# Recurrence of a state space mixer: order of drives, turned inputs and kernel products, and the last state additions handed to TensorE

## The chip, the cores and the metric

One Trainium2 chip, one of its cores. The metric is the device time of one execution in microseconds; lower is better.

## What is computed

Two transformer-like blocks on 256 positions of width 1024, all in float32. The change touches only the first mixer of the first block, a diagonal complex state space model (S5): 512 inner channels in 32 groups of 16, each group with 64 complex states.

```python
u = (h @ w_in).reshape(bsz, seq, SSM_GROUPS, SSM_CH)
mag = jnp.exp(lr * dt)
abar_re = mag * jnp.cos(li * dt)
abar_im = mag * jnp.sin(li * dt)
bu_re = jnp.einsum('bsgc,gpc->bsgp', u, bbar_re)
bu_im = jnp.einsum('bsgc,gpc->bsgp', u, bbar_im)
_, _, xs_re, xs_im = lax.associative_scan(combine, (a_re, a_im, bu_re, bu_im), axis=1)
# y = real part of (c * xs) plus d_skip * u, then gelu, a gate, and w_out
```

After it come a squared-ReLU MLP, an attention mixer with a top-k index, another MLP, and the second block (an SSD branch, windowed attention, a gated MLP). All of that follows in order behind the mixer and is the same before and after.

## The kernel before

The program is written out per engine: each engine has one hand-written stream, in which every instruction stands where it will run, and semaphores (`pe.wait_ge(S(name), n)`, `.then_inc(S(name), 1)`) tie the streams. Nothing reorders them. Weights stream in as numbered pieces in a ring: SyncE loads a piece into `raw`, ScalarE rounds it to `HI`, VectorE and GpSimd make the rest `LO = raw - HI`, and TensorE multiplies with both. `keep_busy(o, n)` issues n products of zeros (bf16, 512 columns) that write into an unused PSUM stretch; they compute nothing.

The recurrence is done in chunks of CL = 4 steps, so there are NC = 64 chunks, and 16 pairs of groups (`ST` tiles) in four quarters q of four tiles. Its steps, with the engine and the names:

- `ch_major` (TensorE): the two pieces of `ssm_w_in`, which give the channels `u`. `to_steps` (ScalarE) rearranges them into `ush`, and SyncE spreads them with 32 small transfers (line 375) into `u5` (in the tile `y`): sixteen for the first half of the channels (`u5_in0`), sixteen for the second (`u5_in1`).
- `inputs_turned(g)` (TensorE, line 778): four transposes of a quarter of the input weights `w5`; `inputs_out` (ScalarE, line 1545) copies them out to `wt5`. Eight such g, through two PSUM banks, so that g waits for the copy of g - 2.
- `drive(q)` (TensorE, line 785): eight products that give the inputs of the chunk states of quarter q.
- `kernels5` (TensorE, line 794): 32 products that give the kernels inside a chunk, with a last product that adds the skip term (line 798, `kk_psum`). ScalarE copies them to `m5` (line 1590, ten copies, `m5_ready`), behind its copies of `cq5` (line 1581), of which the second pair waits for both `u5_in0` and `u5_in1`, since `cq5` lies over `ush`.
- `scanned(q)` (VectorE, lines 2192 to 2202): ten instructions. Two turn the inputs by the angles in `e5`, two add, two are the scans along the chunks, two turn the states back into four products (`ra` and `rb`, 512 columns each), and two (lines 2201 and 2202) add those in pairs to the real and the imaginary part. Then `x5_ready`.
- `within(q)` (TensorE, line 806): the outputs of a chunk from its own inputs, after `m5_ready`. `carried(q)` (TensorE, line 814): the outputs from the state carried into the chunk, after `x5_ready`; 32 products on 32 columns of the array each.
- Gelu on ScalarE (line 1602), the gate `glu`, and the two pieces of `ssm_w_out` (`down`, line 707), then the norm and the first MLP.

What decides the order around the change is thus the text of the TensorE, ScalarE and VectorE streams, and SyncE's single queue of 32 transfers.

## Time and profile before

| | us |
|---|---|
| median of 3 runs (1314.05 to 1314.8) | 1314.8 |
| the profiled execution, its own time | 1318.43 |
| its span | 1316.6 |
| TensorE busy | 1256.2 (95%) |
| VectorE busy | 950.8 (72%) |
| ScalarE busy | 672.3 (51%) |
| GpSimd busy | 424.5 (32%) |
| mean granted TensorE clock | 0.986 of full |

The span runs from the first to the last instruction of the profiled execution; its own time is 1.8 us longer, and taken with the profiler on. The mixer's recurrence lies in the first 92 us of the span. Busy shares are means over the whole program, and say little on so short a stretch; the views of single stretches do. Times within a view are microseconds from the start of the span.

### The profile page before, as it was taken

To read this page: it belongs to the slowest core of one execution; us is meant where nothing else is said; L and a number is where in the kernel's file an instruction comes from. 1 tells how busy PE (TensorE), PEld (TensorE's weight loads), DVE (VectorE), ACT (ScalarE), POOL (GpSimd) and SP (SyncE) were. 2 spreads that over 40 slices of the span, in tenths; PEclk is the share of its full clock that TensorE was granted. 3 is DMA by queue.
4 is the path that set the end of the run, shared out by engine and by line. 5 is a ranking of instruction groups with operands and counts; after the bars stand their busy time and mean duration, and the time that the engine had idled before them with its cause. 6 is when DMAs were issued, how large, how long until landed. Compare 5 with 4: busy or idle time off the path is not lost.

```text
span 1316.6 us, 21079 instructions
## 1 busy us (share of the span) xinstructions
PE 1256.2 (95%) x7823; PEld 1072.4 (81%) x7850; DVE 950.8 (72%) x1439; ACT 672.3 (51%) x1103; POOL 424.5 (32%) x217
## 2 busy tenths in 40 slices
PE   6999999998889999999999999999999999999998
PEld 5866888876667688888788888798999967899997
DVE  7776777676775665556686755468999875799997
ACT  5565444444455444444464544356556643555553
POOL 3014444544211455554344322100000013344543
PEclk9999999999989999999999999999999999999999
DMA  7045665645212566665366533255445514366663
GB/s 231 16 140 182 187 196 178 199 143 175 81 65 80 163 193 191 188 190 150 114 222 192 160 97 97 65 147 161 150 151 159 160 62 146 104 190 189 191 190 112
DMA packets 168927, 197.61 MB, mean 150 GB/s; under 512 B 12542, under 2 KB 133886, under 8 KB 168830
## 3 DMA queue, kind: packets, MB, share of 16 engines
q1 hardware_dynamic: 167499, 192.01, 47.6%
q10 hardware_dynamic: 1362, 4.74, 1.0%
q8 instruction: 41, 0.67, 0.2%
q14 instruction: 25, 0.20, 0.0%
HBM read 195.14 MB, written 1.05 MB: 149 GB/s over the span
## 4 chain that ended last, share of the span: by engine, by line
PE 74%; DVE 13%; DMA 5%; ACT 5%; issue 2%; POOL 1%; SPq 0%; DVEq 0%; ACTq 0%
PE acc L707 23%; PE wk L659 9%; PE wk L621 7%; PE wk L622 7%; PE wk L623 7%; PE wk L661 5%; DMA raw<-in_w_in 2%; DVE LO L475 2%; PE wk L1193 1%; ACT HI L1438 1%; PE acc L926 1%; PE acc L1219 1%; PE acc L621 1%; PE acc L622 1%; PE acc L623 1%
## 5 line engine op out<-in xcount | busy, mean ns | idle before, releaser
L475 POOL TENSOR_TENSOR LO<-raw,HI 128x1024 fp32r<-128x1024 f32 (+1 forms) x158 | 393.4, 2496 | 568.8 <-ACT HI L1438 500.0
L1438 ACT ACTIVATE HI<-raw 128x1024 fp32r<-128x1024 f32 (+3 forms) x382 | 366.1, 995 | 132.9 <-PE acc L707 38.7
L475 DVE TENSOR_TENSOR LO<-raw,HI 128x1024 fp32r<-128x1024 f32 (+1 forms) x156 | 222.7, 1431 | 84.6 <-ACT HI L1438 84.2
L621 PE MATMUL wk<-X,HI 128*128 128x256 f32 x784 | 225.2, 287 | 4.1 <-ACT arena L1872 1.7
L622 PE MATMUL wk<-X,HI 128*128 128x256 f32 x784 | 222.5, 284 | 0.0
L623 PE MATMUL wk<-X,LO 128*128 128x256 f32 x784 | 222.4, 284 | 0.0
L659 PE MATMUL wk<-X,HI 128*128 128x512 f32 x512 | 183.7, 401 | 2.5 <-DVE X L2024 2.5
L621 PEld LDWEIGHTS wk<-X,HI 128*128 128x128 f32 x784 | 150.8, 192 | 7.9 <-issue 3.3
L622 PEld LDWEIGHTS wk<-X,HI 128*128 128x128 f32 x784 | 150.9, 193 | 1.0
L623 PEld LDWEIGHTS wk<-X,LO 128*128 128x128 f32 x784 | 150.9, 193 | 0.0
L661 PE MATMUL wk<-X,LO 128*128 128x256 f32 x512 | 144.1, 281 | 0.0
L707 PE MATMUL acc<-HI,HH 128*128 128x512 f32 x392 | 122.5, 394 | 0.7 <-DVE HL L2518 0.7
L707 PE MATMUL acc<-LO,HH 128*128 128x512 f32 x392 | 121.2, 390 | 0.0
L707 PE MATMUL acc<-HI,HL 128*128 128x512 f32 x392 | 120.9, 390 | 0.0
L659 PEld LDWEIGHTS wk<-X,HI 128*128 128x128 f32 x512 | 96.9, 189 | 26.6 <-issue 2.9
L661 PEld LDWEIGHTS wk<-X,LO 128*128 128x128 f32 x512 | 97.3, 190 | 1.1
L1991 DVE TENSOR_TENSOR LO<-raw,HI 128x1024 fp32r<-128x1024 f32 x68 | 80.2, 1219 | 10.9 <-ACT HI L1438 10.3
L621 PE MATMUL wk<-HI,X 128*128 128x512 f32 x208 | 83.5, 401 | 4.2 <-DVE X L2024 4.2
L707 PEld LDWEIGHTS acc<-LO,HH 128*128 128x128 f32 x392 | 73.6, 188 | 16.0
L707 PEld LDWEIGHTS acc<-HI,HL 128*128 128x128 f32 x392 | 73.6, 188 | 15.8
L2277 DVE TENSOR_TENSOR HL<-arena,HH 128x512 fp32r<-128x512 f32 x32 | 84.0, 2625 | 2.8 <-ACT HH L1635 2.8
L622 PE MATMUL wk<-LO,X 128*128 128x512 f32 x208 | 81.8, 393 | 0.0
(393 smaller groups left out, 2077.1 us busy)
## 6 DMA issues: line engine op xcount, KB each, us to landing
raw<-in_mlp_w SPq DMA_DIRECT2D x128, 512.0 KB, 4.1
raw<-in_w_in SPq DMA_DIRECT2D x100, 512.0 KB, 4.4
raw<-in_w_up SPq DMA_DIRECT2D x44, 512.0 KB, 4.0
raw<-in_w_down SPq DMA_DIRECT2D x44, 256.0 KB, 3.2
raw<-in_att_w_in SPq DMA_DIRECT2D x16, 512.0 KB, 4.1
raw<-in_w_ssd_proj SPq DMA_DIRECT2D x16, 512.0 KB, 3.6
raw<-in_att_w_out SPq DMA_DIRECT2D x8, 512.0 KB, 3.6
raw<-in_w_out SPq DMA_DIRECT2D x8, 512.0 KB, 4.1
```

The source lines that it names most:

```text
L475: tensor_tensor(LO[:, s, cs], raw[:, s % 2, "ab".index(part), 0:m], HI[:, s, cs].bitcast(F32), ALU.subtract).then_inc(S(f"lo_{part}"), 1)
L621: mm(o, lh, rh, start=start, stop=False, skip_group_check=skip)
L622: mm(o, lh, rl, start=False, stop=False, skip_group_check=skip)
L623: return mm(o, ll, rh, start=False, stop=stop, skip_group_check=skip)
L659: mm(o, HI[:, s, w:w + P], X2[:, k, :, :].rearrange("p r t -> p (r t)"), start=k == 0, stop=False, skip_group_check=True)
L661: last = mm(o[:, 0:SEQ], LO[:, s, w:w + P], XH[:, k, :], start=False, stop=k == KD - 1, skip_group_check=True)
L707: last = mm(acc[:, tb, n * 512:(n + 1) * 512], lhs[:, ts], w[:, s, c:c + 512], start=begin, stop=end, skip_group_check=True)
L926: last = mm(acc[:, tb, n * 512:(n + 1) * 512], lhs[:, par, kk, ts], w[:, slots[par], c:c + 512], start=False, stop=end, skip_group_check=True)
L1193: last = mm(wkf[:, o:o + K], qT2[hs, gi * 4 + hd // 2, tb * P:(tb + 1) * P], kT2[hs, gi * 4 + hd // 2, 0:K], start=True, stop=True)
L1438: A(HI[:, s, j * m:(j + 1) * m], raw[:, s % 2, j, 0:m], ACT.Copy).then_inc(S(f"hi_{part}"), 1)
L1991: TT(LO[:, s, cs], raw[:, s % 2, "ab".index(part), :], HI[:, s, cs].bitcast(F32), ALU.subtract).then_inc(S(f"lo_{part}"), 1)
L2277: TT(HL[:, par, :, :], sq_b[:, par, :].rearrange("p (j t) -> p j t", j=2), HH[:, par, :, :].bitcast(F32), ALU.subtract).then_inc(S("hid_lo ...
```

## The change

TensorE's stream: the two first `inputs_turned` no longer stand inside the second `ch_major` but behind it, and the eight are taken as pairs by quarter (real and imaginary part of q together) instead of all real ones first. Between the pairs stand drives and quarters of `kernels5`, with two of the `keep_busy` products that stood there left. Drives 0 and 1 and all of `kernels5` stand ahead of drives 2 and 3; 18 `keep_busy` products follow drive 3, where 8 did. `carried(q)` takes four products per state instead of two sums: 64 instructions instead of 32. VectorE's `scanned(q)` loses its two last additions, and the copy of a plane of `e5` (line 2179) goes too. ScalarE makes the three planes of `e5` with one Copy more, ahead of six of the eight `inputs_out`, and all eight of them now stand ahead of the `cq5` copies. The exponential of `alog` moves from ahead of the first Gelu to behind the `z2_hi` copies.

```diff
@@ -770,7 +770,7 @@
             def inputs_turned(g):
-                r, q = g // 4, g % 4
+                q, r = g // 2, g % 2
                 pe.wait_ge(S("w5_ready"), r + 1)
                 if g >= 2:
                     pe.wait_ge(S("bt_ready"), g - 1)
@@ -786,15 +786,16 @@
                                   u5[:, 4 * q + a, :], start=True, stop=True)
                 last.then_inc(S("bu_psum"), 1)
-            def kernels5(half):
-                for i in range(8 * half, 8 * half + 8):
-                    keep_busy(spare5, 1)
+            def kernels5(q):
+                for i in range(4 * q, 4 * q + 4):
                     for r in range(2):
                         mm(accf[:, 1536 + i * 32:1568 + i * 32], w5[:, r, i, :], ct5[:, r, i, :], start=(i == 0 and r == 0),
                            stop=False, skip_group_check=True)
-                if half == 0:
-                    return
+            def skip_added():
+                pe.wait_ge(S("dd5_ready"), 1)
                 mm(accf[0:32, 1536:2048], ident[0:32, 0:32], dd5.rearrange("p i n -> p (i n)"), start=False, stop=True,
                    skip_group_check=True).then_inc(S("kk_psum"), 1)
@@ -809,11 +810,11 @@
             def carried(q):
                 pe.wait_ge(S("x5_ready"), q + 1)
-                for o, r in itertools.product(range(CL), range(2)):
+                for o, r, part in itertools.product(range(CL), range(2), range(2)):
                     for j in range(4):
                         last = mm(accf[32 * j:32 * j + 32, Y5[q] + o * NC + 1:Y5[q] + (o + 1) * NC],
-                                  cq5[:, r, 4 * q + j, 32 * o:32 * o + 32], lp[:, q, r, j * NC:(j + 1) * NC - 1],
-                                  start=False, stop=(r == 1), skip_group_check=True)
+                                  cq5[:, r, 4 * q + j, 32 * o:32 * o + 32], lp[:, q, r, part * 256 + j * NC:part * 256 + (j + 1) * NC - 1],
+                                  start=False, stop=(r == 1 and part == 1), skip_group_check=True)
                 last.then_inc(S("x5_used"), 1)
             def glu(s, k):
@@ -830,31 +831,34 @@
             spare5 = accf[:, 1024:1536]
-            def first_inputs():
-                pe.wait_ge(S("ct_ready"), 1)
-                pe.wait_ge(S("cols_ready"), 2)
-                inputs_turned(0)
-                inputs_turned(1)
-            used(ch_major(arrived(), 1, between=first_inputs))
-            for g in range(2, 8):
-                keep_busy(spare5, 2)
-                inputs_turned(g)
+            def turned_pair(q):
+                inputs_turned(2 * q)
+                inputs_turned(2 * q + 1)
+            used(ch_major(arrived(), 1))
+            pe.wait_ge(S("ct_ready"), 1)
+            pe.wait_ge(S("cols_ready"), 2)
+            turned_pair(0)
+            kernels5(0)
+            keep_busy(spare5, 2)
+            turned_pair(1)
             pe.wait_ge(S("u5_in0"), 16 * 16)
+            drive(0)
+            kernels5(1)
+            turned_pair(2)
+            pe.wait_ge(S("bt_ready"), 4)
+            drive(1)
+            kernels5(2)
+            turned_pair(3)
+            kernels5(3)
+            skip_added()
+            pe.wait_ge(S("u5_in1"), 16 * 16)
+            pe.wait_ge(S("bt_ready"), 8)
+            drive(2)
             keep_busy(spare5, 2)
-            pe.wait_ge(S("bt_ready"), 8)
-            drive(0)
-            keep_busy(spare5, 1)
-            drive(1)
-            kernels5(0)
-            pe.wait_ge(S("dd5_ready"), 1)
-            kernels5(1)
-            pe.wait_ge(S("u5_in1"), 16 * 16)
-            for q in range(2, 4):
-                keep_busy(spare5, 1)
-                drive(q)
-            keep_busy(spare5, 8)
+            drive(3)
+            keep_busy(spare5, 18)
             pe.wait_ge(S("m5_ready"), 1)
             pe.wait_ge(S("m5_zero"), 3)
             for q in range(4):
@@ -1540,9 +1544,10 @@
                 last.then_inc(S("w5_ready"), 1)
             def inputs_out(first, end):
-                for r, q in ((g // 4, g % 4) for g in range(first, end)):
-                    act.wait_ge(S("bt_psum"), 4 * r + q + 1)
-                    A(wt5[:, 4 * q:4 * q + 4, r, :], wk[:, 2 + q % 2, :].rearrange("p (a n) -> p a n", a=4), ACT.Copy)\
+                for g in range(first, end):
+                    q, r = g // 2, g % 2
+                    act.wait_ge(S("bt_psum"), g + 1)
+                    A(wt5[:, 4 * q:4 * q + 4, r, :], wk[:, 2 + r, :].rearrange("p (a n) -> p a n", a=4), ACT.Copy)\
                         .then_inc(S("bt_ready"), 1)
             act.wait_ge(S("ct_psum"), 1)
@@ -1563,15 +1568,16 @@
                 last = A(cols[:, 1 + r, 0:n], wk[:, 3, r * P:r * P + n], ACT.Copy)
             last.then_inc(S("cols_ready"), 1)
             padded(1)
+            to_steps(1)
             inputs_out(0, 2)
-            to_steps(1)
-            inputs_out(2, 4)
             act.wait_ge(S("angle5_part"), 3)
             A(e5[:, :, 2, :], e5[:, :, 1, :], ACT.Abs).then_inc(S("turn5_abs"), 1)
-            A(e5[:, :, 1, :], e5[:, :, 1, :], ACT.Sin, scale=float(2 * np.pi))
+            steps.link(A(e5[:, :, 0, :], e5[:, :, 1, :], ACT.Sin, scale=float(2 * np.pi)))
             act.wait_ge(S("turn5_abs"), 1)
-            A(e5[:, :, 0, :], e5[:, :, 2, :], ACT.Sin, scale=float(-2 * np.pi), bias=sm5[:, 12, 0:1]).then_inc(S("e5_ready"), 1)
-            inputs_out(4, 8)
+            A(e5[:, :, 1, :], e5[:, :, 2, :], ACT.Sin, scale=float(-2 * np.pi), bias=sm5[:, 12, 0:1]).then_inc(S("turn5_abs"), 1)
+            act.wait_ge(S("turn5_abs"), 2)
+            A(e5[:, :, 2, :], e5[:, :, 0, :], ACT.Copy, scale=-1.0).then_inc(S("e5_ready"), 1)
+            inputs_out(2, 8)
             for r in range(2):
                 act.wait_ge(S("q5_half"), r + 1)
                 if r == 1:
@@ -1592,9 +1598,6 @@
             act.wait_ge(S("q5_ready"), 1)
             load_gpre(1)
             hi_to(3)
-            act.wait_ge(S("late_in"), 16 * N_LATE)
-            A(alog[:, :], alog[:, :], ACT.Exp).then_inc(S("alog_ready"), 1)
             for first, end in ((0, 2), (2, 3), (3, 4)):
                 act.wait_ge(S("x5_used"), end)
                 act.wait_ge(S("x5_ready"), end)
@@ -1617,6 +1620,8 @@
                 A(XH[:, 4 + 2 * b:6 + 2 * b, :].rearrange("p q (c t) -> p q c t", t=CL),
                   z2f[:, 2 * b:2 * b + 2, :].rearrange("p q (t c) -> p q c t", t=CL), ACT.Copy, scale=0.5)\
                     .then_inc(S("z2_hi"), 1)
+            act.wait_ge(S("late_in"), 16 * N_LATE)
+            A(alog[:, :], alog[:, :], ACT.Exp).then_inc(S("alog_ready"), 1)
             hi_to(6)
             post(1, 4)
@@ -2176,7 +2181,6 @@
                 link(TT(grid(qb), by_power(pw5[:, 1, 1:5, :]), every_power(cc5[:, 1 - r, :, :]), ALU.mult))
                 TT(qa, qa, qb, ALU.add if r == 0 else ALU.subtract).then_inc(S("q5_half"), 1)
             dve.wait_ge(S("e5_ready"), 1)
-            link(V.tensor_copy(e5[:, :, 2, :], e5[:, :, 0, :]))
             dve.wait_ge(S("mag4_ready"), 1)
             def planes(t):
@@ -2188,18 +2192,16 @@
                 ps = slice(4 * q, 4 * q + 4)
                 ra, rb, z = lp[:, q, 0, :], lp[:, q, 1, :], z5
                 bu = wk[:, q, :].rearrange("p (a r c) -> p r a c", a=4, r=2)
-                ea, eb = (e5[:, ps, n:n + 2, :].rearrange("p a r c -> p r a c") for n in range(2))
+                eb, ea = (e5[:, ps, n:n + 2, :].rearrange("p a r c -> p r a c") for n in range(2))
                 TT(planes(ra), bu, ea, ALU.mult)
                 link(TT(planes(rb), bu, eb, ALU.mult))
-                TT(ra[:, 0:256], ra[:, 0:256], ra[:, 256:512], ALU.add)
+                TT(ra[:, 0:256], ra[:, 0:256], ra[:, 256:512], ALU.subtract)
                 link(TT(rb[:, 0:256], rb[:, 256:512], rb[:, 0:256], ALU.subtract))
                 mag = mag4[:, ps, :].rearrange("p a c -> p (a c)")
                 V.tensor_tensor_scan(z[:, 0:256], mag, ra[:, 0:256], 0.0, ALU.mult, ALU.add)
                 link(V.tensor_tensor_scan(z[:, 256:512], mag, rb[:, 0:256], 0.0, ALU.mult, ALU.add))
                 TT(planes(ra), planes(z), ea, ALU.mult)
-                link(TT(planes(rb), planes(z), eb, ALU.mult))
-                TT(ra[:, 0:256], ra[:, 0:256], ra[:, 256:512], ALU.subtract)
-                TT(rb[:, 0:256], rb[:, 0:256], rb[:, 256:512], ALU.add).then_inc(S("x5_ready"), 1)
+                TT(planes(rb), planes(z), eb, ALU.mult).then_inc(S("x5_ready"), 1)
             def z_low(first, end):
                 bs = slice(first, end)
```

TensorE, from the end of the second input projection to its first gate products: L621 to L623 are the projection, L778 the transposes, L686 `keep_busy`, L785 a drive, L794 and L798 kernel products and skip term before the change. The piece below, in the order before, is from the last transposes to the first kernel products; the pattern of its last two rows goes on until all 16 tiles are done.

```order
L778 MATMUL wk<-cst,arena 128x128 x4
L686 MATMUL acc<-zero_bf 128x512 x2
L778 MATMUL wk<-cst,arena 128x128 x4
L686 MATMUL acc<-zero_bf 128x512 x2
L785 MATMUL wk<-y,arena 128x64 x8
L686 MATMUL acc<-zero_bf 128x512
L785 MATMUL wk<-y,arena 128x64 x8
L686 MATMUL acc<-zero_bf 128x512
L794 MATMUL acc<-arena 128x32 x2
L686 MATMUL acc<-zero_bf 128x512
L794 MATMUL acc<-arena 128x32 x2
```

The same stretch of TensorE after the change, from the first transposes to the skip term; L793 and L799 are what L794 and L798 were.

```order
L778 MATMUL wk<-cst,arena 128x128 x8
L793 MATMUL acc<-arena 128x32 x8
L686 MATMUL acc<-zero_bf 128x512 x2
L778 MATMUL wk<-cst,arena 128x128 x8
L785 MATMUL wk<-y,arena 128x64 x8
L793 MATMUL acc<-arena 128x32 x8
L778 MATMUL wk<-cst,arena 128x128 x8
L785 MATMUL wk<-y,arena 128x64 x8
L793 MATMUL acc<-arena 128x32 x8
L778 MATMUL wk<-cst,arena 128x128 x8
L793 MATMUL acc<-arena 128x32 x8
L799 MATMUL acc<-arena,cst 32x512
```

What moved: the transposes left the projection, kernel products now stand between transposes and drives in fours of tiles, and drives 2 and 3 come behind the skip term. The next piece is TensorE right behind drive 3, at the chunk outputs (L806 and L807 `within`, L814 and L815 `carried`), before:

```order
L785 MATMUL wk<-y,arena 128x64 x8
L686 MATMUL acc<-zero_bf 128x512 x8
L806 MATMUL acc<-y,arena 32x64 x16
...
L806 MATMUL acc<-y,arena 32x64 x16
L686 MATMUL acc<-zero_bf 128x512
L814 MATMUL acc<-arena 32x63 x32
L686 MATMUL acc<-zero_bf 128x512
```

TensorE at the same place after the change:

```order
L785 MATMUL wk<-y,arena 128x64 x8
L686 MATMUL acc<-zero_bf 128x512 x18
L807 MATMUL acc<-y,arena 32x64 x16
...
L807 MATMUL acc<-y,arena 32x64 x16
L686 MATMUL acc<-zero_bf 128x512
L815 MATMUL acc<-arena 32x63 x64
L686 MATMUL acc<-zero_bf 128x512
```

The filler behind the drives grew, and each carried step doubled its products, with the same shapes. On ScalarE, around the input copies (L1545 and L1550 `inputs_out`, L1570 to L1573 and L1574 to L1579 the planes of `e5`, L1581 and L1587 `cq5`), before:

```order
L1545 ACTIVATE arena<-wk 128x4x128 x2
L1531 ACTIVATE arena<-wk 128x512
L1545 ACTIVATE arena<-wk 128x4x128 x2
L1570 ACTIVATE arena<-arena 128x16x64
L1571 ACTIVATE arena<-arena 128x16x64
L1573 ACTIVATE arena<-arena 128x16x64
L1545 ACTIVATE arena<-wk 128x4x128 x4
L1581 ACTIVATE arena<-arena,cst 128x64x16 x2
L1581 ACTIVATE arena<-gpre,cst 128x64x16 x2
L1590 ACTIVATE arena<-acc 32x16x32 x10
```

ScalarE at the same place after the change, with one row of the other projection ahead:

```order
L1535 ACTIVATE arena<-wk 128x512
L1550 ACTIVATE arena<-wk 128x4x128 x2
L1574 ACTIVATE arena<-arena 128x16x64
L1575 ACTIVATE arena<-arena 128x16x64
L1577 ACTIVATE arena<-arena 128x16x64
L1579 ACTIVATE arena<-arena 128x16x64
L1550 ACTIVATE arena<-wk 128x4x128 x6
L1587 ACTIVATE arena<-arena,cst 128x64x16 x2
L1587 ACTIVATE arena<-gpre,cst 128x64x16 x2
```

The planes of `e5` now stand ahead of six of the input copies, and a fourth instruction joins them.

## Rows read from the trace of the kernel before

**Rows 1.** The chain of waits that ended last, 60 to 90 us: start, length, what.

```profile
61.06 0.98 PE acc L798 x2
...
68.10 0.65 PE acc L806 x32
...
71.79 1.02 PE acc L814 x64
...
75.64 1.02 PE acc L814 x64
...
83.67 1.06 PE acc L814 x64
84.76 0.39 ACT arena L1602
```

**Rows 2.** Timeline of TensorE: start, length, line, count of records, idle before.

```profile
34.55 1.03 PE L778 MATMUL wk<-cst,arena 128*128 128x128 f32 x8
...
38.52 0.38 PE L686 MATMUL acc<-zero_bf 128*128 128x512 bf16 x1
...
44.40 0.63 PE L778 MATMUL wk<-cst,arena 128*128 128x128 f32 x4 [2.02 <-ACT arena L1545]
...
51.83 0.53 PE L794 MATMUL acc<-arena 128*128 128x32 f32 x4
...
62.19 3.84 PE L785 MATMUL wk<-y,arena 128*128 128x64 f32 x32
65.86 1.89 PE L686 MATMUL acc<-zero_bf 128*128 128x512 bf16 x8
...
73.06 0.52 PE L814 MATMUL acc<-arena 128*32 128x63 f32 x21 [0.25 <-issue]
73.83 0.85 PE L814 MATMUL acc<-arena 128*32 128x63 f32 x43 [0.24 <-issue]
```

**Rows 3.** The 32 transfers into `u5`: issue times and lengths in ns, time to landing.

```profile
L375 SPq DMA_DIRECT2D y<-arena x32: 593/597/1117, 30.8 to 51.3; - x32
...
DMA to landing us min/median/max: 1.8/1.8/2.6
```

**Rows 4.** Timeline of ScalarE, 40 to 95 us.

```profile
46.70 0.60 ACT L1545 ACTIVATE arena<-wk 128x512 f32<-128x512 f32 x1 [1.04 <-PE wk L778]
47.20 2.17 ACT L1581 ACTIVATE arena<-arena,cst 128x1024 f32<-128x1024 f32 x2
53.21 2.19 ACT L1581 ACTIVATE arena<-gpre,cst 128x1024 f32<-128x1024 f32 x2 [3.84 <-DMA y<-arena]
...
73.53 1.28 ACT L1602 ACT_TABLE_LOAD   x1
...
92.46 1.06 ACT L1438 ACTIVATE HI<-raw 128x1024 fp32r<-128x1024 f32 x1 [0.93 <-DMA raw<-in_mlp_w]
```

**Rows 5.** Timeline of VectorE, 45 to 95 us.

```profile
45.18 0.69 DVE L2179 COPY arena<-arena 128x1024 f32<-128x1024 f32 x1
49.97 0.69 DVE L2192 TENSOR_TENSOR arena<-wk,arena 128x512 f32<-128x512 f32 x1 [4.10 <-PE wk L785]
...
54.72 0.42 DVE L2201 TENSOR_TENSOR arena<-arena 128x256 f32<-128x256 f32 x1
...
83.03 0.42 DVE L2202 TENSOR_TENSOR arena<-arena 128x256 f32<-128x256 f32 x1
...
93.95 1.22 DVE L475 TENSOR_TENSOR LO<-raw,HI 128x1024 fp32r<-128x1024 f32 x1
```

**Rows 6.** Windows: length, busy us of each engine (count), granted clock, DMA share, GB/s.

```profile
41.60:45.00 3.40, 1.38 (x11) 0.85 (x9) 3.33 (x4) 3.15 (x5) 0.00 (x0) 1.00 0.12 24
45.00:48.40 3.40, 3.40 (x14) 2.22 (x12) 0.86 (x2) 2.29 (x4) 0.00 (x0) 0.50 0.13 29
...
62.10:65.50 3.40, 3.35 (x30) 3.35 (x31) 1.35 (x3) 3.34 (x6) 2.82 (x3) 1.00 0.00 0
...
113.30:116.70 3.40, 3.23 (x10) 2.77 (x11) 2.37 (x4) 3.40 (x4) 1.41 (x1) 0.51 0.85 302
```

## The prediction

> **What bounds the kernel now.** I read the chain of waits that ended last first, because busy shares over 1316 us say nothing on a stretch of 60 us. Between 60 and 90 us it alternates: the skip term on TensorE ends at 62.04, then ten ScalarE copies into `m5` fill the time until `within` starts at 68.10, then TensorE alone leads through `within`, the carried steps at 71.79 and 75.64, the gate products, and the last carried step at 83.67, after which Gelu starts at 84.76 [rows 1]. So two things set the end of the recurrence: when `m5` is ready, and the sum of TensorE's work behind it. Next the timelines of the three engines. TensorE stood idle for 2.02 us before 44.40, since the copies of the turned inputs stood behind the `e5` instructions on ScalarE, and its first kernel product came at 51.83 [rows 2]. ScalarE had its `cq5` copies done at 55.40, the second pair having waited 3.84 us for the transfers into `u5`, and from 55.40 to 62.06 it waited for TensorE [rows 4, 1]. VectorE waited 4.10 us for drive 0 and began at 49.97 [rows 5].
>
> **Part 1, `m5` earlier.** What is due first is drive 0, and it needs the first sixteen transfers. 32 are issued evenly from 30.8 to 51.3, one each 0.66 us, and each lands 1.8 us after its issue [rows 3]: the sixteenth at 30.8 + 15 x 0.66 + 1.8 = 42.5, the last at 53.1. Nothing in the change moves these. TensorE's projection ended by 38.5; without eight transposes (1.03, of which 0.15 overlaps) it ends at 37.6 [rows 2]. Then come transposes, a quarter of the kernel products, two fillers and transposes, until 41.3, and TensorE idles some 1.2 us for the transfers. From 42.5 on it runs drive 0, kernels, transposes, drive 1, kernels, transposes. Prices: two drives with a filler between took 3.84, and a filler 0.22 (eight in 1.89), so 1.85 a drive [rows 2]; sixteen tiles of kernel products with sixteen fillers took 61.06 - 51.83 = 9.23, so 0.58 a tile, 0.36 without the filler, 1.45 a quarter [rows 1, 2]; eight transposes 0.87. The sum is 2 x (1.85 + 1.45 + 0.87) = 8.3, and the last transposes end at 50.8, with 0.2 for seams at 51.0. ScalarE's copies keep up: its planes of `e5` are three instructions on 1024 columns and now a fourth, at the 1.05 that each such copy into `cq5` takes [rows 4], from 39.1 to some 43.4, and the next transposes ask for a copy only at 45.8.
>
> Behind 51.0 ScalarE has a last input copy (0.5 until the next may start), two pairs of `cq5` copies of 2.1 (the second could start at 53.7, after 53.1, so it no longer waits), and the ten `m5` copies, which took 62.04 to 68.10 = 6.05 [rows 1, 4]. 51.0 + 0.1 + 0.5 + 4.2 + 6.0 = 61.8. The skip term ends on TensorE at 51.0 + 1.45 + 0.98 = 53.4, before ScalarE asks for it at 55.8; drives 2 and 3 with fillers (3.7 + 0.4 + 3.9) end at 61.5. So `within` starts at 61.8 in place of 68.10: **-6.3 us**. What is late next is ScalarE's queue: all eight input copies stand ahead of `cq5`, and the last of them waits for TensorE's last transposes.
>
> **Part 2, VectorE's scans.** Drive 0 ends at 44.4; VectorE is free at 45.2, when its copy of an `e5` plane used to start [rows 5]. A scan took 49.97 to 55.4; without the two additions, which start at 54.72, it is 4.7 [rows 5]. Scans 0 and 1 end at 50.0 and 54.7, scan 2 at 60.0 (drive 2 ends at 55.3). All are done before the first carried step at 61.8 + 3.7 = 65.5. These savings are therefore worth nothing on the first three steps. If part 1 failed to bring `within` forward they would be worth nothing either, since scans were ahead of `m5` already.
>
> **Part 3, the carried steps doubled.** Each had 64 records in 1.02 us, save the second, which took 73.06 to 74.68 = 1.62 with a hole of 0.24 in it [rows 1, 2]. 64 more records of one shape should cost 1.02 each, and TensorE leads from `within` to the last of them, so all four are on the path; I take 1.05 each: **+4.2 us**. The low bound is 0.9 each, if the fixed tail of a step is not doubled (+3.6); the high bound is the rate of the second, 1.62 each, below.
>
> The one place where a scan led too is the last step: the additions end at 83.03 + 0.42 = 83.45, and the step starts at 83.67 [rows 1, 5]. From the end of the third step (76.66) TensorE's own work fills 7.0 us until then. VectorE's way over that stretch gets 0.7 shorter, so TensorE alone sets it and nothing is gained or lost. The end of the fourth step thus moves by -6.3 + 4.2 = **-2.1 us**.
>
> **Part 4, at no cost.** The exponential and its table load leave the place before the first Gelu, where they ended with Gelu's own load (73.53 + 1.28 = 74.81) just as the second carried step did [rows 4]; the load that is left finds ScalarE idle. At the new place, after the Gelu gate, they take 1.5 us ahead of a weight piece whose rounding was waiting for its transfer (0.93 of idle before 92.46) and whose low part VectorE takes only at 93.95 [rows 4, 5]; the first half would be rounded at 93.1 by the old clock. The cover is about 0.8 us; without it up to 1.5 would be lost. From there on the stages move together, 2.1 us earlier, and the loads with them.
>
> **The sum.** The profiled execution took 1318.43, 3.6 above the median of the runs shown. 1318.43 - 2.1 = 1316.3, and against the median 1314.8 - 2.1 = **1312.7 us**.
>
> **Rival 1, TensorE slows at the tiny products (+2.0 us).** If all four doubled steps ran at the rate of the one with the hole (25 ns a record instead of 16), they would take 4 x 3.24 = 13.0 where the four took 3 x 1.02 + 1.62 = 4.7: +8.3, and with -6.3 the kernel is 2.0 slower, 1316.8. It decides against the change from (4.7 + 6.3) / 4 = 2.75 us a step. For it: the hole, put down to issue, which may be the fetching of instructions, and the stream is twice as dense. Against: the other three steps in the trace show no hole [rows 1].
> The Trainium skill ("TensorE: Matmul & The Clock Gate", section "Wait — 56ns, not 53.3ns?") says that matmuls never start closer than about 25 ns apart however small they are; an estimate by that page is 3.2 us a step and a kernel 1.8 us slower. The trace disagrees for three steps of four, with 1.02 us for 64 records, and agrees for the piece of 21 records in 0.52 us [rows 1, 2].
>
> **Rival 2, the clock halves in the new stretch (-0.5 us).** After TensorE had been busy for only 1.38 of 3.40 us, the granted clock was 0.50 from 45.00 to 48.40; after 3.35 of 3.40 busy with drives it stayed at 1.00 [rows 6]. 0.50 is the lower level, 1.2 GHz. The change leaves an idle stretch of 1.2 us before drive 0 and takes out nearly all fillers until 57. A stretch of 3.4 us at half clock before 51.0 costs 1.7 us of TensorE work on the path: -6.3 + 1.7 + 4.2 = -0.4, 1314.3.
>
> **Rival 3, more than forecast (-3.8 us).** The granted clock was 0.51 from 113.30 to 116.70 too, in the first MLP's products behind the norm's waits [rows 6], and where these waits fall changes when all moves by 2 us. One such stretch avoided is another -1.7, 1311.0.
>
> **Rival 4, the change does not do what it says.** If ScalarE's queue or the transfers hold `m5` back, part 1 shrinks and part 3 stays: with `m5` only 4.2 earlier it is 0, and at none, +4.2. The arrival times above leave little room for it.
>
> **Chances.** Forecast with its own range 1311.8 to 1313.8: 0.46. Rival 1: 0.12, rival 2: 0.17, rival 3: 0.20, rival 4: 0.05. About 0.2% (2.6 us) is what a measurement of this kernel can tell from no change; -2.1 is inside it, but near its edge. Faster by more: rival 3, most of the lower third of the forecast: 0.36. Slower by more, where a carried step takes over 3.4 us or rival 4 holds fully: 0.07. Within: 0.57. The range runs from rival 3 to rival 1, less its far end: 1310.6 to 1316.2.
>
> **What would show it.** `within` starting at 61.8 (part 1), ScalarE's second `cq5` pair without a wait for transfers, carried steps of 2.05 to 2.1 us with 128 records each, no wait of TensorE for VectorE before the fourth, Gelu after it at 82.6, and the first piece of the last projection 2.1 earlier than now. A carried step of 3 us is rival 1; a granted clock of 0.5 between 42 and 55 is rival 2. The forecast is wrong if TensorE waits at a carried step, or if the norm behind the mixer gives back the time in waiting for a weight piece.

## The result and the profile after

The changed kernel took 1334.87 us (median of 4 runs, 1332.33 to 1334.99), the kernel before beside it 1314.45 (4 runs, 1314.05 to 1314.8): 20.4 us between the medians and a ratio of 1.0148 [1.0132, 1.0164], so 1.5% slower, where 2.1 us less was forecast. The profiled execution took 1334.99, with a span of 1333.2, and so is 16.6 longer than the profiled one of before, which lay 4.0 above its median. The traces can account for the 16.6; the other 3.8 of the 20.4 stand in no trace. The mean granted clock was 0.976, where it was 0.986. In the experiments, which ran on other chips of the same kind, 15 of 74 executions of the kernel before took 1328.6 to 1338.88 us at a mean clock of 0.972 to 0.977, and two of it and one of a kernel below took 1609 us or more at 0.727 or less; the ratios leave out most of these, and so differ a little from the quotient of the medians. So the kernel before loses some clock too, in a fifth of its executions; no trace of such an execution was kept, and where in the program it loses it is open.

TensorE's timeline of the changed kernel answers to [rows 2] and [rows 1]:

```profile
43.45 2.69 PE L785 MATMUL wk<-y,arena 128*128 128x64 f32 x16 [1.41 <-DMA y<-arena]
45.93 3.57 PE L793 MATMUL acc<-arena 128*128 128x32 f32 x16
49.31 1.95 PE L778 MATMUL wk<-cst,arena 128*128 128x128 f32 x8
51.05 3.51 PE L785 MATMUL wk<-y,arena 128*128 128x64 f32 x16
...
62.87 1.91 PE L799 MATMUL acc<-arena,cst 32*32 32x512 f32 x2
64.71 3.68 PE L785 MATMUL wk<-y,arena 128*128 128x64 f32 x16
69.03 3.51 PE L785 MATMUL wk<-y,arena 128*128 128x64 f32 x16
72.33 5.51 PE L686 MATMUL acc<-zero_bf 128*128 128x512 bf16 x18
77.78 0.65 PE L807 MATMUL acc<-y,arena 128*32 128x64 f32 x32
...
81.40 1.67 PE L815 MATMUL acc<-arena 128*32 128x63 f32 x105
83.46 0.53 PE L815 MATMUL acc<-arena 128*32 128x63 f32 x23 [0.38 <-issue]
84.25 1.64 PE L815 MATMUL acc<-arena 128*32 128x63 f32 x104 [0.25 <-issue]
87.20 0.54 PE L815 MATMUL acc<-arena 128*32 128x63 f32 x24 [1.31 <-issue]
...
98.51 1.97 PE L815 MATMUL acc<-arena 128*32 128x63 f32 x128
```

The order is the one that was planned: drive 0 (line 785) after 1.41 us of idling for its transfers, a quarter of the kernel products (line 793), transposes (778), drive 1. But from drive 0 to drive 3 nearly every duration is doubled. Drive 1 took 3.51 us where 1.85 was reckoned, a quarter of the kernel products 3.57 where 1.45 was reckoned, `within` starts at 77.78 instead of 61.8. The windows say why (same columns as [rows 6], granted clock third from the end, behind GpSimd's busy time):

```profile
41.16:44.56 3.40, 1.99 (x19) 1.75 (x17) 3.33 (x4) 3.34 (x5) 0.00 (x0) 1.00 0.11 24
44.56:47.98 3.42, 3.42 (x18) 3.42 (x18) 2.21 (x5) 0.34 (x1) 0.00 (x0) 0.50 0.12 25
71.87:75.28 3.41, 3.41 (x11) 1.52 (x11) 3.41 (x4) 3.39 (x5) 0.00 (x0) 0.50 0.00 0
75.28:78.70 3.42, 3.17 (x47) 1.59 (x46) 0.14 (x1) 0.73 (x1) 0.00 (x0) 1.00 0.82 279
```

The granted clock fell to 0.50 (1.2 GHz) at 44.6, in the middle of drive 0, and came back at 75.3, among the 18 `keep_busy` products behind drive 3: 30.7 us in one piece. Before, the same stretch had one piece of 3.4 [rows 6]. TensorE was busy for 3.20 or more of every 3.40 us in it.

ScalarE and VectorE follow TensorE, and do not lead:

```profile
50.44 0.60 ACT L1550 ACTIVATE arena<-wk 128x512 f32<-128x512 f32 x1 [5.54 <-PE wk L778]
...
58.87 0.60 ACT L1550 ACTIVATE arena<-wk 128x512 f32<-128x512 f32 x1 [6.97 <-PE wk L778]
...
60.21 2.17 ACT L1587 ACTIVATE arena<-arena,cst 128x1024 f32<-128x1024 f32 x2
62.29 2.17 ACT L1587 ACTIVATE arena<-gpre,cst 128x1024 f32<-128x1024 f32 x2
64.81 3.58 ACT L1596 ACTIVATE arena<-acc 32x512 f32<-32x512 f32 x6 [0.35 <-PE acc L799]
...
68.41 2.38 ACT L1596 ACTIVATE arena<-acc 32x512 f32<-32x512 f32 x4
```

The ten `m5` copies (line 1596) were done at 70.8, and yet `within` began at 77.78. What lay between is TensorE's own queue: the end of drive 3 and the 18 fillers, most of them at half clock, 5.51 us. These fillers were meant to pass the time until `m5` is ready; here they stood on the path from their first to their last. The second pair of `cq5` copies (line 1587) no longer waits for transfers, as the prediction had it.

The account of the 16.6 us of span, from these rows and [rows 1]: `within` starts 77.78 - 68.10 = 9.7 later; from there to the end of the fourth carried step it takes 100.48 - 77.78 = 22.7 where it took 84.73 - 68.10 = 16.6, so 6.1 more. That makes 15.8, and the rest of the program differs by 0.8. The 9.7 are two things: drive 0 started at 43.45 where 42.5 was reckoned, still at full clock, since its transfers were issued from 31.3 on and not from 30.8; the rest came after the fall.

### The profile page after: what moved, and what is told of

It is laid out like the page before. It is cut to its first block, busy times and chain, and to the rows that moved or that the text cites. A ratio compares the mean times of both kernels' runs of the same rounds, so it can differ in the third digit from the quotient of the medians.

```text
span 1333.2 us, 21548 instructions
## 1 busy us (share of the span) xinstructions
PE 1273.2 (95%) x8062; PEld 1086.9 (82%) x8087; DVE 973.3 (73%) x1430; ACT 670.8 (50%) x1103; POOL 410.0 (31%) x217
## 3 DMA queue, kind: packets, MB, share of 16 engines
HBM read 195.14 MB, written 1.05 MB: 147 GB/s over the span
## 4 chain that ended last, share of the span: by engine, by line
PE 83%; DVE 7%; ACT 3%; DMA 3%; issue 2%; POOL 1%; SPq 1%; DVEq 0%; ACTq 0%
PE acc L707 23%; PE wk L621 9%; PE wk L659 9%; PE wk L622 9%; PE wk L623 9%; PE wk L661 5%; PE acc L621 1%; PE wk L1197 1%; PE acc L930 1%; PE acc L1223 1%; PE acc L622 1%; PE acc L623 1%; PE acc L686 1%; PE wk L686 1%; PE wk L785 1%
## 5 line engine op out<-in xcount | busy, mean ns | idle before, releaser
L475 POOL TENSOR_TENSOR LO<-raw,HI 128x1024 fp32r<-128x1024 f32 (+1 forms) x158 | 378.6, 2403 | 596.2 <-ACT HI L1442 555.5
L475 DVE TENSOR_TENSOR LO<-raw,HI 128x1024 fp32r<-128x1024 f32 (+1 forms) x156 | 252.2, 1620 | 82.8 <-ACT HI L1442 82.5
L621 PE MATMUL wk<-X,HI 128*128 128x256 f32 x784 | 225.8, 288 | 3.3 <-ACT arena L1877 1.7
L623 PE MATMUL wk<-X,LO 128*128 128x256 f32 x784 | 223.0, 285 | 0.0
L621 PEld LDWEIGHTS wk<-X,HI 128*128 128x128 f32 x784 | 151.6, 193 | 6.9 <-issue 3.3
L623 PEld LDWEIGHTS wk<-X,LO 128*128 128x128 f32 x784 | 151.7, 194 | 0.0
L621 PE MATMUL wk<-HI,X 128*128 128x512 f32 x208 | 83.5, 401 | 4.2 <-DVE X L2029 4.2
```

The costliest lines, as they stand in the source:

```text
L475: tensor_tensor(LO[:, s, cs], raw[:, s % 2, "ab".index(part), 0:m], HI[:, s, cs].bitcast(F32), ALU.subtract).then_inc(S(f"lo_{part}"), 1)
L621: mm(o, lh, rh, start=start, stop=False, skip_group_check=skip)
L623: return mm(o, ll, rh, start=False, stop=stop, skip_group_check=skip)
```

## The experiments

Two theories stood against each other on the first term. **Clock**: the new order is worth what was reckoned, and the half clock, which comes because the fillers are gone (and because TensorE idles ahead of drive 0), costs it back. **Chain**: the new order is slow in itself, since transposes, copies and drives wait for one another. On the second term: **products** (64 more of them at 16 ns) against **supply** (a dense stream of small records runs into holes).

### The new order alone

The changed kernel with the recurrence's sums on VectorE again, and `e5` as before:

```diff
-                for o, r, part in itertools.product(range(CL), range(2), range(2)):
+                for o, r in itertools.product(range(CL), range(2)):
...
+                TT(ra[:, 0:256], ra[:, 0:256], ra[:, 256:512], ALU.subtract)
+                TT(rb[:, 0:256], rb[:, 256:512], rb[:, 0:256], ALU.add).then_inc(S("x5_ready"), 1)
```

> The changed kernel with the second part undone: carried steps of 32 instructions, VectorE's additions and its copy back; order and fillers as changed. Theory: the clock falls at 44.6 as in the changed kernel, `within` starts at 77 to 78 (9.7 later than before), no hole in the carried steps, and the kernel takes 9 to 12 us more than before; together with the run of the other part alone it adds up to the 20 us of the change. Rival (the loss in time behind `within` is also the order's): over 15 us more than before.

Measured: five executions, sorted by the mean clock: 1313.11 us at 0.990, then 1325.49 (0.980), 1322.36 (0.978), 1326.02 (0.976) and 1331.85 (0.974). The ratio of the median is 1.0068 [1.0043, 1.0094], which is 9 us, at the lower end of what was expected; but the clock did not fall in all five. The one at 0.990, 9 to 19 us faster than the four others, is the one that was profiled:

```profile
42.54 2.00 PE L785 MATMUL wk<-y,arena 128*128 128x64 f32 x16 [1.50 <-DMA y<-arena]
44.38 1.92 PE L793 MATMUL acc<-arena 128*128 128x32 f32 x16
46.13 1.07 PE L778 MATMUL wk<-cst,arena 128*128 128x128 f32 x8
47.04 1.90 PE L785 MATMUL wk<-y,arena 128*128 128x64 f32 x16
...
58.21 4.05 PE L686 MATMUL acc<-zero_bf 128*128 128x512 bf16 x18
62.35 0.65 PE L807 MATMUL acc<-y,arena 128*32 128x64 f32 x32
```

```profile
43.40:46.80 3.40, 3.40 (x33) 3.40 (x32) 3.33 (x5) 0.00 (x0) 0.00 (x0) 1.00 0.12 24
46.80:50.20 3.40, 3.40 (x34) 3.40 (x32) 3.30 (x7) 1.08 (x2) 0.00 (x0) 1.00 0.12 24
```

This is the same stream as in the changed kernel up to `within`, in an execution in which the clock stayed up. Drives take 1.9, kernel quarters 1.9 (1.75 from start to start), and `within` starts at 62.35, 5.75 ahead of before; its span is 5.3 shorter. The chain theory falls: nothing in the order waits much more than was reckoned. Against it, `within` in the changed kernel came 15.4 us later, at 77.78. Of these, 0.9 lie ahead of drive 0 (43.45 against 42.54, with the first transfer issued at 31.3 against 30.3), before the clock fell; the other 14.5 are the half clock. TensorE's busy share does not tell the two apart: 3.40 of 3.40 here at clock 1.00, 3.42 of 3.42 there at 0.50. And the idle time ahead of drive 0 does not decide it alone either, since it was 1.50 in this one.

### The carried steps alone

The kernel before, with the four products per state on TensorE and nothing else moved; the fourth `e5` instruction comes with it:

```diff
-                for o, r in itertools.product(range(CL), range(2)):
+                for o, r, part in itertools.product(range(CL), range(2), range(2)):
...
+            A(e5[:, :, 2, :], e5[:, :, 0, :], ACT.Copy, scale=-1.0).then_inc(S("e5_ready"), 1)
...
-                TT(ra[:, 0:256], ra[:, 0:256], ra[:, 256:512], ALU.subtract)
-                TT(rb[:, 0:256], rb[:, 256:512], rb[:, 0:256], ALU.add).then_inc(S("x5_ready"), 1)
+                TT(planes(rb), planes(z), eb, ALU.mult).then_inc(S("x5_ready"), 1)
```

> The kernel before with the second part of the change alone: the states' four products go to TensorE, 64 instructions a carried step in place of 32, VectorE's two additions and its copy gone. Theory: `within` starts at 68.1 as before, the steps take 2.0 us each and some have holes of 0.4 to 1.3 us from issue, as in the changed kernel (1.67 + 0.53 with 0.38 between, 1.64 + 0.54 with 1.31 between): 4 to 7 us slower than before. Rival (the holes come of the changed order, not of the number of instructions): no holes, 4 us slower.

Measured: five executions from 1320.68 to 1327.2 and a sixth of 1344.2 at a mean clock of 0.973; ratio 1.0065 [1.004, 1.0089], 8.6 us, somewhat over the 4 to 7 expected; the profiled span is 7.2 over that of before. Its timeline of TensorE (the line is 814 here):

```profile
73.10 1.41 PE L814 MATMUL acc<-arena 128*32 128x63 f32 x86
74.97 0.82 PE L814 MATMUL acc<-arena 128*32 128x63 f32 x42 [0.46 <-issue]
...
79.25 0.85 PE L814 MATMUL acc<-arena 128*32 128x63 f32 x43 [1.81 <-issue]
...
90.52 1.97 PE L814 MATMUL acc<-arena 128*32 128x63 f32 x128
```

`within` began at 69.47 in place of 68.10, because transposes waited 3.26 us for ScalarE's copies instead of 2.02 [rows 2]. The first three steps have holes of 0.46, 1.81 and 0.37 after some 80 records, 2.64 together, where before there was one of 0.24 [rows 2]. The fourth, which has the long products of the output projection before it, has none: 1.97 for 128 records, where the timeline of before has 1.09 for 64, so 0.88 more.

To tell whether the holes belong to the products or to what stands close around them, the same kernel with ten fillers ahead of each of the first three steps:

```diff
-            for q, n in enumerate((0, 1, 4)):
+            for q, n in enumerate((10, 10, 10)):
```

> The kernel before with the carried steps doubled, and ten fillers (2.2 us, few instructions) ahead of each of the first three steps in place of 0, 1 and 4. Theory (the holes in a doubled step are TensorE waiting for instructions that it takes faster than they are fetched): with the long fillers between, the holes of 0.46, 1.81 and 0.37 us go or shrink below 0.3 in sum, and the steps take 2.0 us each. Rival (the holes come of the step's own products, their columns or banks): holes of the same size at the same place, after 80 to 105 records.

Measured once, 1330.66 us (the span is 4.8 over that of the kernel without the added fillers). Its timeline of TensorE:

```profile
73.87 1.97 PE L814 MATMUL acc<-arena 128*32 128x63 f32 x128
...
78.03 2.19 PE L814 MATMUL acc<-arena 128*32 128x63 f32 x128
...
82.42 1.97 PE L814 MATMUL acc<-arena 128*32 128x63 f32 x128
```

No hole is left, though each step has the same 128 records. So a hole is not a property of the 128 products, but depends on what stands before them. A rule for when it comes does not follow. The first doubled step of the kernel with both fillers below has none either, 128 records in 2.05 us behind one filler, while steps of only 64 records had holes of 0.84 and 0.96 us after 40 and 22 of them (the order alone, and the kernel with half its fillers below). The profile puts the idle time down to issue; that instructions arrive too slowly there fits, but no view shows the arrival of instructions, so that part is argued, not shown.

### Fillers back into the new order

Three kernels take the whole change and put back one filler per tile of kernel products (A), six ahead of drive 0's wait (B), or both:

```diff
                 for i in range(4 * q, 4 * q + 4):
+                    keep_busy(spare5, 1)
...
             turned_pair(1)
+            keep_busy(spare5, 6)
             pe.wait_ge(S("u5_in0"), 16 * 16)
```

A alone:

> The changed kernel with one filler product (512 columns of zeros) ahead of each of the 16 tiles of kernel products, as the kernel before had. Theory 1 (the loss up to the start of `within` is the granted clock, which fell to 0.50 at 44.6 us and came back only at 75.3): the clock stays at 1.00 from 44 to 64, `within` starts at 63 to 64 in place of 77.8, and the kernel takes 1315 to 1318. Theory 2 (the new order itself, with ScalarE's queue and the handshake of transposes and copies, is slow): the clock may stay up, but `within` starts later than 70 and the kernel stays over 1325.

B alone:

> The changed kernel with six filler products (1.3 us) in the one place where TensorE idled for 1.41 us, ahead of drive 0; the rest stays without fillers. Theory 1a (that idle stretch alone took the clock down): the clock stays at 1.00, `within` starts at 62 to 63, the kernel takes 1314 to 1316. Theory 1b (the stream of drives, transposes and small kernel products without fillers takes the clock down whatever is ahead of it): the clock falls a little later, by 48 to 51, stays down until the fillers behind drive 3, and the kernel stays within 3 us of 1335.

Both:

> The whole change with both sets of fillers: one ahead of every tile of kernel products and six ahead of drive 0. Theory: no mean clock under 0.985 in any run, `within` at 64 to 65 (3.5 earlier than before), doubled steps with holes of 1 to 3 us in sum (+5 to +7): 1.5 to 3.5 us slower than before. Rival (the second part is also what takes the clock down): runs at a clock of 0.98 or less remain, 10 us slower and more.

| kernel | executions | mean clock | median us | ratio to before |
|---|---|---|---|---|
| A, a filler per tile | 10 | eight at 0.989 to 0.993, two at 0.980 and 0.983 | 1320.59 | 1.0048 [1.0022, 1.0074] |
| B, six ahead of drive 0 | 4 | 0.980 to 0.985 | 1327.69 | 1.0099 [1.007, 1.0128] |
| both | 10, one of them left out | 0.987 to 0.991 | 1320.45 | 1.0025 [0.9997, 1.0052] |

The one left out of the last row took 1609.15 us at a mean clock of 0.727; the kernel before had two such beside the changed one (0.556 and 0.653), so it is not put down to the fillers. With A the two executions at the low clock took 1332.11 and 1329.1, the eight others 1317.74 to 1321.25; `within` began at 64.56. The median and this start lie somewhat over what was expected (1315 to 1318, and 63 to 64). With B alone the clock still fell, later: at 56.2 instead of 44.6, for 10.2 us, and most of the fillers behind drive 3 fell into it. That is neither of the two expectations: it fell later than 48 to 51, and the median is 7 us under the changed kernel's. TensorE's timeline:

```profile
55.15 2.78 PE L785 MATMUL wk<-y,arena 128*128 128x64 f32 x16
...
61.88 6.29 PE L686 MATMUL acc<-zero_bf 128*128 128x512 bf16 x18
68.09 0.65 PE L807 MATMUL acc<-y,arena 128*32 128x64 f32 x32
```

With both, the mean clock stayed at 0.987 or over in the nine. TensorE's timeline of that kernel:

```profile
64.35 0.65 PE L808 MATMUL acc<-y,arena 128*32 128x64 f32 x32
...
67.97 2.05 PE L816 MATMUL acc<-arena 128*32 128x63 f32 x128
...
73.45 0.86 PE L816 MATMUL acc<-arena 128*32 128x63 f32 x46 [1.78 <-issue]
...
76.92 0.96 PE L816 MATMUL acc<-arena 128*32 128x63 f32 x50 [0.40 <-issue]
```

`within` is 3.75 ahead of before and the carried steps give that back and more. So the whole change with its clock held is 0.25% slower or the same, and the clock makes up the rest: some 16 us of the 1.48%, or 11 us if the changed kernel's second ratio, 1.0107 in the last experiment, is taken. The 14.5 of the traces lie between.

The 18 fillers behind drive 3 cost something here too. ScalarE had `m5` ready at 63.83, and `within` waited another 0.5 us for TensorE's fillers to end, as it did in the three kernels with the sums on VectorE below.

### The kernel before, without its fillers

The same suspicion, tried in the old order: only the 16 fillers among the kernel products go, nothing is added or moved.

```diff
                 for i in range(8 * half, 8 * half + 8):
-                    keep_busy(spare5, 1)
```

> The kernel before with only the 16 fillers among the kernel products taken out, its order and everything else kept. They take 3.5 us, and `m5` waits for the kernel products here, so with the clock held `within` starts at 64.6 and the kernel is 3.5 us faster. Theory (fillers hold the clock in this stream, in whatever order): in several runs the half clock that began at 45 lasts longer than 3.4 us, mean clocks of 0.98 and less appear, and the median gains less than 3.5 or loses. Rival (only the new order lets the clock fall): mean clocks as before, 3 to 4 us faster.

Measured: ten executions, 1321.36 to 1328.03, all at a clock of 0.979 to 0.984; ratio 1.0051 [1.0029, 1.0074]. Taking out the 16 fillers, 3.5 us at 0.22 each, made the kernel 6.7 us slower. `within` began at 74.37 instead of 68.10. Timeline and windows of TensorE:

```profile
51.09 10.52 PE L793 MATMUL acc<-arena 128*128 128x32 f32 x64
61.53 1.91 PE L797 MATMUL acc<-arena,cst 32*32 32x512 f32 x2
...
70.82 3.62 PE L686 MATMUL acc<-zero_bf 128*128 128x512 bf16 x8
74.37 1.01 PE L805 MATMUL acc<-y,arena 128*32 128x64 f32 x32
```

```profile
50.20:53.60 3.40, 3.40 (x33) 3.40 (x33) 3.30 (x7) 0.00 (x0) 0.00 (x0) 1.00 0.12 24
57.00:60.40 3.40, 3.40 (x18) 3.40 (x17) 3.31 (x6) 0.00 (x0) 0.00 (x0) 0.50 0.00 0
```

TensorE did nothing but kernel products from 51.09 to 61.5 and was busy all the time; the clock fell at 54.7 and came back at 75.2. Its last wait had ended at 47.30, 7.4 us before the fall, and the longer one of 2.02 us at 45.12. So the stream of small products loses the clock here without a wait in front of it; with fillers among them the same kernel kept it in 19 of the 25 executions taken beside these. What the idle time ahead of drive 0 adds is less sure: with fillers in it the fall came later (56.2), but that is one trace, and the order alone kept its clock behind 1.50 us of idling.

### The part that pays, by itself

The new order with the sums on VectorE, and fillers as in the kernel with both:

> The changed kernel's order with the second part undone (carried steps of 32 instructions, VectorE's additions back), one filler ahead of every tile of kernel products and six fillers ahead of drive 0. Theory (the clock is held by fillers both in the wait for the transfers and in the sparse stream behind it): no run has a half clock between 40 and 75 us, the mean clock of every run is 0.985 or more, `within` starts at 64 to 65, 3.5 earlier than before, and the kernel is 3 to 4 us faster than before (0.2 to 0.3%). Rival (the order is at fault even with fillers): some runs at a mean clock of 0.98 or less, and no gain.

The same with a filler only at every second tile in quarters 1 and 2:

```diff
                 for i in range(4 * q, 4 * q + 4):
+                    if q in (0, 3) or i % 2 == 0:
+                        keep_busy(spare5, 1)
```

> As the run with all fillers, but in the two middle quarters of the kernel products, which lie ahead of the last input copies, only every second tile has a filler. Theory: half the fillers still hold the clock in most runs, `within` starts 0.9 us earlier than with all of them, 4 to 5 us faster than before. Rival: the clock falls in some runs and the median is slower than with all fillers.

And that with the fillers between the carried steps set as (0, 4, 1) instead of (0, 1, 4), against the hole of 0.96 us that its second step still had:

> The version of the changed order with sums left to VectorE and half of the fillers, which was 0.4% faster than before, with four of the fillers of the carried steps moved from ahead of the third to ahead of the second step and one left there. Theory: the hole of 0.96 us in its second step goes, since TensorE's instructions are fetched meanwhile: 4 to 6 us faster than before, an interval clear of 1. Rival (the hole moves to another step): the same as without the move, 4 us faster.

| kernel | executions | mean clock | median us | ratio to before |
|---|---|---|---|---|
| a filler per tile | 10 | 0.988 to 0.991 | 1313.39 | 0.997 [0.9938, 1.0001] |
| every second in two quarters | 10 | 0.987 to 0.992 | 1313.24 | 0.9963 [0.9934, 0.9991] |
| that, spread | 12 | 0.986 to 0.991 | 1313.64 | 0.9976 [0.9957, 0.9996] |

None of the 32 executions had a mean clock under 0.986, where 17 of the 74 of the kernel before had one of 0.977 or less. `within` began at 64.48, 63.71 and 64.30, 3.6 to 4.4 ahead of before, and the gains of 3.2 to 4.9 us agree with that, though the intervals are wide and the first touches no change. The spreading took the hole away (64 records in 1.29, behind four fillers), without a gain that can be told; 4 to 6 us were expected and 3.2 measured:

```profile
68.95 1.04 PE L686 MATMUL acc<-zero_bf 128*128 128x512 bf16 x4
69.92 1.29 PE L817 MATMUL acc<-arena 128*32 128x63 f32 x64
```

Against the whole change with the same fillers, leaving the sums on VectorE is worth 1.0025 - 0.997 = 0.55%, 7 us: the price of part 3, with some 4 us of uncertainty in either ratio, which are from two chips.

### The changed kernel again

Nothing edited, to see whether it ever keeps its clock:

> The changed kernel itself, unaltered, in more executions, since in the run with its order alone one execution of five kept a mean clock of 0.99 and took 1313 us while the other four had 0.974 to 0.980 and took 1322 to 1332. Theory (whether the clock falls in the bare stretch is decided anew in each execution): most executions at 0.975 to 0.98 and 1330 to 1336, a few at 0.985 or more and 1318 to 1322. Rival (it always falls in this kernel): all at 0.98 or less.

Six executions, 1326.74 to 1338.52, at 0.974 to 0.981; ratio 1.0107 [1.0049, 1.0164]. With the first four, ten of ten had a low mean clock; the two of them that were profiled show the fall in this stretch. In the second the half clock lasted from 45.4 to 72.7, 27.3 us, and `within` began at 75.64. A mean clock alone does not tell the place: this execution also had 17.1 us of half clock at 400 us, where the first had 6.8. In the order alone one of five had kept it. The two differ in ScalarE's and VectorE's work and in the carried steps, not in TensorE's stream ahead of `within`, so what makes the difference is open, as is whether it is more than chance with five executions against ten.

## Why the prediction was wrong

**The step that failed is the clock in the new stretch, which the forecast put at nothing.** Part 1 reckoned every drive, quarter of kernel products and set of transposes from 42.5 to `within` at the prices of full clock (1.85, 1.45 and 0.87 us), and took the fillers out at a gain. In the changed kernel they ran at half clock, 3.51, 3.57 and 1.95 us. Rival 2, "the clock halves in the new stretch", named the right mechanism and the right place ("a granted clock of 0.5 between 42 and 55 is rival 2"), but was mis-judged in both chance and size. Its chance was 0.17, and against it stood one row of before, 3.35 of 3.40 us busy with drives at clock 1.00 [rows 6]. That row was read as if a busy TensorE kept its clock. But 16 fillers stood among the kernel products before it, and it began with one itself; in the kernel without those 16, a TensorE busy 3.40 of 3.40 lost it. The size was taken as one stretch of 3.4 us, a loss of 1.7, as at 45.00 in the trace of before. In the changed kernel one fall lasted 30.7 us and cost 14.5 on the path.

The long falls ended only where fillers stood in a row: at 75.3 and 72.7 in the two traces of the changed kernel and at 66.4 with B, among the 18 behind drive 3, and at 75.2 in the kernel before without its 16, right behind the 8. With 14.5 in place of nothing the forecast's sum is -6.3 + 14.5 + 4.2 = +12.4. With the other terms as measured, and the 0.9 of drive 0's later start, it is -5.75 + 0.9 + 14.5 + 6.1 = +15.8, which is the account above, told in the prediction's terms and not a check of its own.

The Trainium skill ("TensorE: Matmul & The Clock Gate", section "HAM oscillation — how this bites in real kernels") puts the loss of the clock down to waits for DMA, of 3 to 5 us in its example. These traces agree at most in that 1.41 us of waiting stands ahead of the fall in the changed kernel. They do not for the order alone, which kept its clock behind 1.50 us, nor for the kernel before without its fillers, where the clock fell in a stretch without a gap; there the measurement decides.

**Part 1, right where the clock held.** `within` at 62.35 instead of 61.8, -5.75 instead of -6.3. Drive 0 started at 42.5, `cq5` no longer waited for transfers, and ScalarE kept up. The missing 0.55 is the price of a tile of kernel products without its filler: 0.36 was got by taking 0.22 from 0.58, but 1.75 us for four tiles is 0.44, so a quarter is 0.3 dearer, and two stand on the path. Taking a filler out from among these products thus gained 0.14 us and not 0.22, and the prediction did not ask what it paid for. In the versions with fillers `within` came 1.4 to 2.2 us later than at 62.35.

**Part 2, right.** VectorE's shorter scans were worth nothing on the first three steps: its third scan ended at 73.15, the first carried step began at 81.40. In the changed kernel it waited for drives instead:

```profile
68.42 0.69 DVE L2196 TENSOR_TENSOR arena<-wk,arena 128x512 f32<-128x512 f32 x1 [9.10 <-PE wk L785]
```

**Part 3, mis-sized.** "All four are on the path; I take 1.05 each: +4.2", measured +6.1 in the changed kernel. The products themselves are near what was said (0.80 to 1.16 a step, 3.96 in all). The holes of 0.38, 1.31 and 0.68 us, 2.37 in all, replaced one of 0.24, and the sum had no term for them. Rival 1 had seen the clue in that one hole of before, but gave it the form of a rate of 25 ns for every record, which no step shows: 128 records in 1.97 us are 15 ns each. The Trainium skill ("TensorE: Matmul & The Clock Gate", section "Wait — 56ns, not 53.3ns?") has about 25 ns as the least from start to start; for these products on 32 columns of the array each, the measurement of 15 ns decides.

**Part 4, right.** The exponential at its new place held nothing up: VectorE took the low part of the next weight piece at 109.71 where it was 93.95 [rows 5], 15.8 later, just as the end of the fourth carried step.

Rivals 3 and 4 did not come. The transfers held back drive 0 alone, by the 0.9 us above. The half-clock stretches behind 100 us come mostly in the same places, later by the delay, with one gone, one new and one twice as long; together they are 27.3 us before and 30.7 after.

## What to carry to other kernels

A filler product is a term of the sum like any other. Before one is taken out, or a stream is thinned, ask what holds the granted clock there without it. Price a fall not at one short stretch but until the next row of fillers or other work that brought the clock back in a trace, which here was 30 us away. A busy TensorE is no evidence: read the granted clock of windows that contain only the kind of product that will be left, and if the trace has none, run the old order without fillers first. Small products are cheap one by one, but when their number in a row is doubled, allow for holes: here three doubled steps had 2.4 us of them, beside 4.0 us for the added products of all four.

## What was unexpected of the hardware

The clock stayed at 0.50 with TensorE busy for 3.07 or more of every 3.4 us, mostly all of it, in 20.5 us of the kernel before without its fillers and 30.7 of the changed one, nearly all of it fp32 products and transposes on 32 to 128 columns. One bf16 product of 512 columns ahead of every four records of kernel products, with six more ahead of drive 0, kept the mean clock at 0.987 or over in 19 of 20 executions, of which the 20th is the one of 1609 us. And whether it falls is not the same in each execution: one of five of the order alone and eight of ten with A kept it, and 17 of 74 of the kernel before lost it, each under the same instructions. What decides it is open.
